# Mixture of experts on one core: tokens sorted by group on chip, and the expert weights moved past 128 sorted tokens instead of 256 tokens moved past the weights

## The reference, cut to what matters

```python
def _moe_sublayer(x, ...):                      # 256 tokens, D = 2048
    ht = _rms(x, ffn_norm_g)
    g_prob = softmax(ht @ w_router_group + b)   # 4 groups
    p_group, g_sel = top_k(g_prob, 1)           # one group for each token
    e_logit = (ht @ w_router_expert + b).reshape(T, 4, 4)[arange(T), g_sel]
    top_val, top_idx = top_k(e_logit, 2)        # two of the group's four experts
    w_top = softmax(top_val) * p_group
    ...
    for e in range(16):                         # D_EXPERT = 256
        hid = silu(ht @ w_expert_gate[e]) * (ht @ w_expert_up[e])
        y = y + combine[:, e:e + 1] * (hid @ w_expert_down[e])
    return x + y
```

## Time and profile before

| | |
|---|---|
| median of 3 runs | 3567.73 us (3565.65 to 3570.1) |
| the profiled execution: its own time | 3567.64 us |
| its span, from the first to the last instruction | 3565.8 us |
| mean granted TensorE clock | 0.988 of 2.4 GHz |
| TensorE busy | 3477.7 us, 98% of the span |
| VectorE, ScalarE busy | 1912.3 us (54%), 1482.6 us (42%) |
| HBM read | 593.76 MB, 167 GB/s over the span |

### The profile page before, as it was taken

One profiled execution on the slowest core, in us unless ns is written; L12 is line 12 of the kernel. 1 busy time (PEld: TensorE's weight loads), 2 busy tenths in 40 slices (PEclk: granted clock), 3 DMA queues, 4 the chain that ended last, 5 costly groups with the idle time before them and its releaser, 6 DMA issues.

```text
span 3565.8 us, 64376 instructions
## 1 busy us (share of the span) xinstructions
PE 3477.7 (98%) x27880; PEld 3408.4 (96%) x27880; DVE 1912.3 (54%) x1663; ACT 1482.6 (42%) x1475; POOL 184.4 (5%) x179
## 2 busy tenths in 40 slices
PE   7999989999999999999999999999999999999998
PEld 7898879999999999999999999999988999999998
DVE  6644555555555665555444444454677554545454
ACT  4334444333333467434333333443355443434342
POOL 1140001000000022010000000010000100000001
PEclk9999999899999999999999999999999999999999
DMA  6544335456555544555555555555543566656564
GB/s 187 175 142 130 119 118 165 132 186 188 186 182 186 186 136 148 171 176 179 174 174 176 177 177 175 174 171 165 176 130 111 184 189 188 185 185 186 188 188 142
DMA packets 578957, 598.24 MB, mean 168 GB/s; under 512 B 11728, under 2 KB 565968, under 8 KB 578800
## 3 DMA queue, kind: packets, MB, share of 16 engines
q1 hardware_dynamic: 574752, 588.42, 52.9%
q0 software_dynamic: 1552, 5.92, 0.6%
q10 hardware_dynamic: 2496, 1.56, 0.2%
HBM read 593.76 MB, written 2.10 MB: 167 GB/s over the span
## 4 chain that ended last, share of the span: by engine, by line
PE 87%; DVE 6%; ACT 3%; issue 2%; DMA 1%; SPq 0%; POOL 0%; ACTq 0%; DVEq 0%; POOLq 0%
PE acc L484 26%; PE acc L486 26%; PE acc L488 26%; DVE low L1442 2%; ACT high L1002 1%; PE psx L855 1%; ACT probs L1115 1%; DMA raw<-in_w_in 1%; PE psx L704 1%; PE acc L839 1%; PE psx L839 1%; PE acc L838 1%; PE psx L838 1%; PE psx L840 1%; PE acc L840 1%
## 5 line engine op out<-in xcount | busy, mean ns | idle before, releaser
L1698 DVE TENSOR_TENSOR low<-raw,high 128x2048 fp32r<-128x2048 f32 x374 | 857.1, 2292 | 573.4 <-ACT high L1181 573.1
L484 PE MATMUL acc<-gh,high 128*128 128x256 f32 (+1 forms) x5440 | 1122.0, 288 | 24.6 <-DVE low L1442 20.7
L486 PE MATMUL acc<-gl,high 128*128 128x256 f32 (+1 forms) x5440 | 1104.5, 284 | 0.0
L488 PE MATMUL acc<-gh,low 128*128 128x256 f32 (+1 forms) x5440 | 1103.4, 284 | 0.0
L1181 ACT ACTIVATE high<-raw 128x2048 fp32r<-128x2048 f32 x374 | 714.6, 1911 | 646.4 <-DMA raw<-in_mlp_w 507.8
L484 PEld LDWEIGHTS acc<-gh,high 128*128 128x128 f32 x5440 | 850.0, 190 | 35.0 <-issue 25.1
L486 PEld LDWEIGHTS acc<-gl,high 128*128 128x128 f32 x5440 | 850.1, 190 | 0.0
L488 PEld LDWEIGHTS acc<-gh,low 128*128 128x128 f32 x5440 | 845.2, 189 | 0.0
L1442 DVE TENSOR_TENSOR low<-raw,high 128x2048 fp32r<-128x2048 f32 x180 | 418.4, 2329 | 334.4 <-ACT high L1002 333.7
L1002 ACT ACTIVATE high<-raw 128x2048 fp32r<-128x2048 f32 x180 | 342.8, 1910 | 229.2 <-DMA raw<-in_w_kv 62.6
L484 PE MATMUL acc<-fh,high 128*128 128x272 f32 (+1 forms) x2048 | 414.6, 284 | 0.0
(11 more groups left out here) (339 smaller groups left out, 3052.0 us busy)
## 6 DMA issues: line engine op xcount, KB each, us to landing
raw<-in_mlp_w SPq DMA_DIRECT2D x256, 1024.0 KB, 5.5
raw<-in_w_in SPq DMA_DIRECT2D x60, 1024.0 KB, 5.2
raw<-in_a_w_in SPq DMA_DIRECT2D x40, 1024.0 KB, 5.1
raw<-in_w_expert_gate SPq DMA_DIRECT2D x32, 1024.0 KB, 5.3
raw<-in_w_expert_up SPq DMA_DIRECT2D x32, 1024.0 KB, 5.3
raw<-in_w_expert_down SPq DMA_DIRECT2D x32, 1024.0 KB, 5.4
raw<-in_w_kv SPq DMA_DIRECT2D x32, 1024.0 KB, 5.5
raw<-in_a_w_out SPq DMA_DIRECT2D x20, 1024.0 KB, 5.1
```

Source lines behind the costliest of these rows:

```text
L484: pe.matmul(o[n], hw[:, k, c[n]], h, start=first, stop=False)
L486: pe.matmul(o[n], hw[:, k, c[n]], l, start=False, stop=False)
L488: m = pe.matmul(o[n], lw[:, k, c[n]], h, start=False, stop=last)
L1698: dve.tensor_tensor(low[:, k % SLOTS, :], raw[:, k % SLOTS, :], high[:, k % SLOTS, :].bitcast(F32), ALU.subtract)\
```

## The change

- **Router earlier.** The last steps of `wout` also transpose each finished pair of tiles of `hT` (`turn_tokens`, four 128 x 128 transposes) and do the router's matmuls for it (`router(t)`). ACT takes the transposed tiles as `xth` and their squares' sums (`take_tokens`), DVE the remainders `xtl`.
- **Sort.** Before any expert: DVE picks each token's group; TensorE counts (`count`) the groups and each token's place in its own; DVE orders the groups by size, writes their numbers to `gid`, and makes a one-hot matrix from tokens to sorted places. SP reads `gid` into four registers and only then issues the first expert weights. TensorE multiplies the tokens by the one-hot matrix (`sort`, 64 matmuls of 256 columns), ACT and DVE split the result into `gsh` and `gsl`. The second largest group comes first, then the largest, which lies across the border at place 128, then the other two: so rank 0 has tokens in both halves of 128 places, and each of ranks 1, 2 and 3 in one.
- **Experts.** The 128 sorted tokens are the stationary operand and 256 columns of weights move past. A unit of rank 0 has 48 matmuls of 256 columns, a unit of ranks 1 to 3 has 24. Units come in fours, rank 0, 1, 2, 3. The hidden values come out by tokens and are transposed back (`turn_hidden`).
- **Down.** Again tokens are stationary: 24 matmuls of 512 columns for rank 0 and 12 for each other rank. The loads have rows of 4 KB instead of 1 KB. The result is taken in two halves of the columns, each put back into token order by a matmul with the transposed one-hot matrix (`unsort`, 8 calls of 8 matmuls of 256 columns) and added to `hT`.
- The first two pairs of `a_in` are worked on with their halves interleaved (`A_ORDER`), so that the second half of `hT` is needed two units later. One of the seven sums of squares (`sum_squares`, `stats`) is gone, as are `turn_weights` and `weights_out`.
- The experts and `down` are written out instead of looped.

```diff
-            with sp.Fori(0, NEXP) as i:
-                for j in range(4):
...
+            sp.wait_ge(gid_ready, 1)
+            at_rank = [sp.value_load(gid[0:1, r:r + 1], min_val=0, max_val=NGRP - 1) for r in range(4)]
+            for u in range(64):
+                k, j, q = U0["experts"] + u, u // 16, u % 16
+                sp.wait_ge(unit_done, k - SLOTS + 1)
+                sp.dma_start(raw[:, k % SLOTS, :].rearrange("p (kt n) -> p kt n", n=256),
+                             (vg if q < 8 else vu)[q // 4 % 2, :, ds(at_rank[q % 4] * EPG + j, 1), :, :]
+                             .rearrange("p e kt n -> p (e kt) n")).then_inc(raw_in[k % SLOTS], 16)
...
+        RANKS = [[(0, 0), (1, 1)], [(0, 2)], [(1, 3)], [(1, 4)]]
...
+            def count():
+                pe.wait_ge(grouped, 1)
...
+                pe.matmul(o[:, 0:4], ones[:, :], g0, start=True, stop=False)
+                pe.matmul(o[:, 0:4], ones[:, :], g1, start=False, stop=True)
+                pe.matmul(o[:, 4:8], earlier[:, :], g0, start=True, stop=True)
+                pe.matmul(o[:, 8:12], ones[:, :], g0, start=True, stop=False)
+                pe.matmul(o[:, 8:12], earlier[:, :], g1, start=False, stop=True).then_inc(count_mm, 1)
+            def sort(t):
+                for k in range(2):
+                    c = slice(P * (2 * t + k), P * (2 * t + k) + P)
+                    for n, (i, x) in enumerate(((0, xth), (1, xth), (0, xtl), (1, xtl))):
+                        m = pe.matmul(sort_bank(t)[:, S * k:S * k + S], x[:, i, c], onehot[:, i, :],
+                                      start=n == 0, stop=n == 3)
+                m.then_inc(sort_mm, 1)
...
+            def expert_unit(u):
+                k, j, q = U0["experts"] + u, u // 16, u % 16
+                part, h, r = q // 8, q // 4 % 2, q % 4
+                pe.wait_ge(lo_ready, k + 1)
...
+                for kk in range(8):
...
+                    for s, x in RANKS[r]:
+                        o = bank_of(x)[:, 256 * part:256 * part + 256]
+                        a, b = gsh[:, kt, P * s:P * s + P], gsl[:, kt, P * s:P * s + P]
+                        pe.matmul(o, a, hw[:, kk, :], start=kt == 0, stop=False)
+                        pe.matmul(o, b, hw[:, kk, :], start=False, stop=False)
+                        m = pe.matmul(o, a, lw[:, kk, :], start=False, stop=kt == KT - 1)
+                    if kk == 3:
+                        if u == 5:
+                            turn_onehot()
+                        elif u == 7:
+                            sort_values()
+                        elif q == 15:
+                            turn_hidden(5 * j), turn_hidden(5 * j + 1)
+                        elif j and q < 3:
+                            turn_hidden(5 * j - 3 + q)
+                m.then_inc(unit_done, 1)
...
+            def down_unit(u):
...
+                for f in range(2):
+                    for s, x in RANKS[r]:
+                        a, b = hidh[:, x, j, f, :], hidl[:, x, j, f, :]
...
+                        for n in range(2):
+                            pe.matmul(down_bank(c, s, n), a, hw[:, f, 512 * n:512 * n + 512], start=first, stop=False)
...
+                    elif f == 0 and 18 <= u < 22:
+                        unsort(u - 18)
...
             for u in range(40):
                 k = U0["a_in"] + u
...
+                def mid():
+                    if u == 0:
+                        for t in range(4, 8):
+                            unsort(t)
```

On DVE the start of the experts reads:

```diff
+            for t in range(4):
+                sorted_low(t)
+            lo_c(U0["experts"])
+            sorted_low(4), sorted_low(5)
+            lo_c(U0["experts"] + 1)
+            sorted_low(6), sorted_low(7)
...
+            for u in range(64):
+                j, q = u // 16, u % 16
+                lo_c(U0["experts"] + u + 2)
+                if u == 0:
+                    shares()
+                elif u == 1:
+                    slot_values()
```

More of the change, by code:

```diff
@@ L776, in router @@
[L776 to L788, removed]
-                    m = pe.transpose(psx[0:NEXP, 3, P * i:P * i + P], comb[:, i, :], ident)
-                m.then_inc(comb_t, 1)
@@ L804, in expert @@
-            def expert(i):
-                for j in range(4):
-                    k = U0["experts"] + j
-                    fresh = isinstance(i, int)
-                    unit(i * 4 + k, k % SLOTS, j % 2, 2, B0["experts"] + j // 2, lambda kt: gh2[:, kt, :],
-                         lambda kt: gl2[:, kt, :], free=i * 2 + (B0["experts"] + j // 2 - 1),
-                         need=need_g(8) if fresh and j < 2 else None, mid=turn_weights if fresh and j == 2 else None)
-                    if fresh and j == 0:
-                        router()
-                    if fresh and j >= 2:
-                        weights_out(j - 2)
@@ new lines, in router @@
+            def router(t):
+                if t == 0:
+                    pe.wait_ge(rg_ready, 1)
+                for i in range(2):
+                    for kt in (2 * t, 2 * t + 1):
+                        m = pe.matmul(psx[:, 2 + i, 0:20], hT[:, kt, META + P * i:META + P * i + P], rg[:, kt, :],
+                                      start=kt == 0, stop=kt == KT - 1)
+                if t == 7:
+                    m.then_inc(rl_mm, 1)
+            for u in range(16):
+                k, t = U0["wout"] + u, u // 2
+                def mid():
+                    if u == 0:
+                        heads_out(NKV - 1)
+                    elif u % 2 == 0:
+                        turn_tokens(t - 1), router(t - 1)
+                unit(k, k % SLOTS, u % 2, 2, B0["wout"] + t, lambda kt: yh[:, kt, :], lambda kt: yl[:, kt, :],
+                     free=B0["wout"] + t - 1, need=need_y if t == 0 else None, mid=mid)
@@ L820, in need_hid @@
+            for u in range(32):
+                down_unit(u)
             def need_hid(base):
@@ L1242, in _, with sorted_hi @@
-            expert(0)
-            with act.Fori(0, NEXP - 1) as i:
-                expert(i + 1)
-            resid_stage("down", 2, 4, 2, "g_a", gh3, ALL)
-            hi_c(U0["a_in"] + 2)
-            root(2, TB)
+            def sorted_hi(t):
+                act.wait_ge(sort_mm, t + 1)
+                for k in range(2):
+                    m = act.activation(gsh[:, 2 * t + k, :], sort_bank(t)[:, S * k:S * k + S], ACT.Copy,
+                                       scale=col("g_ffn", 2 * t + k))
+                m.then_inc(g_hi, 1)
@@ L1250, in _ @@
+            for n in range(4):
+                take_sorted(1, n)
+            hi_c(U0["a_in"] + 2)
+            for t in range(4, 8):
+                resid(t, t, t % 2, 1, 2, "g_a", gh3, ALL)
+                if t == 5:
+                    hi_c(U0["a_in"] + 3)
+            root(1, TB)
             act.wait_ge(lam_z, 1)
@@ L1822, in _ @@
+            lo_c(U0["a_in"] + 2)
+            add_back(4), add_back(5)
+            for t in range(4, 8):
+                if t < 6:
+                    add_back(t + 2)
+                g_low(t, "g_a", gh3, gl3, ALL, 16 + t + 1)
+                if t == 6:
+                    lo_c(U0["a_in"] + 3)
+            root(1, TB)
             half_log, z, s_, s2, p_ = (rc[:, k, :] for k in (0, 2, 3, 4, 5))
```

541 lines of the change are left out of this document (382 added, 159 removed).

## The result

The changed kernel takes 3429.93 us (median of 4 runs, 3429.1 to 3436.9), the kernel before took 3568.91 in runs beside it: ratio 0.9615, 95% interval 0.9601 to 0.9629. It is 139 us faster. The forecast was 3422 us, 8 us less. The profiled execution took 3430.53 us with a span of 3428.7; all that follows is read from it.

A forecast was written before the change was run, and what follows sets the result against it. TensorE, 98% busy, was taken as the bound. wout 15.0, start 52.7, other units 226.0, down 123.3 and end 5.8 make 422.8 us in place of 568.1, giving span 3420.5 and time 3422 us, range 3385 to 3480.

The forecast's parts named there:

- `wout`: `wout` stage: seven of eight tile pairs' transposes and router matmuls inside it, at 0.18 us each, add 15 us, nothing hiding them.
- start to the end of unit 4: From the last `wout` matmul through five expert units: 19.7 us of matmuls plus 33.0 bare, 52.7 us.
- the other 59 units: Gate and up after unit 4: 205.7 us of matmuls, 14.75 waits of 1.27 and 1.6 for transposes, 226.0 us.
- down: Down: eight fours of 15.24 us, each with a 1.44 us wait, plus 1.4 for `unsort` and `turn_hidden`, 123.3 us.
- end: `unsort`, recurrent block: First `a_in` units: 3.8 us for the second half of `unsort`, recurrent DVE chain about 2 us later, 5.8 us.
- The bound changes hands: Gate and up: rank 0's slot needs 9.72 us, TensorE has 8.45 of work, so it waits 1.27 us every four units.
- Rival 1: Gate, up and down: landing under 4.0 us brings slots round within 8.4, waits go, TensorE stays bound; 3392 us, chance 0.12.
- The period of four: Gate and up: four units, one of each rank, take 15.35 us including TensorE's wait for rank 0's slot.
- Bare time: Start of the experts: TensorE time not covered by the first five units' matmuls, 33 us, range 25 to 44.
- rival 2: Experts and down: the clock falls at each wait, 1.7 us in each of 24 fours; 3463 us, chance 0.15.

The follow-up runs named there:

- e8_rows: Changed kernel with gate and up loads giving each partition 8 KB of adjacent rows instead of 8 rows of 1 KB: 3415.81 us (one run).
- e6_router: Changed kernel with all 64 router matmuls behind the last matmul of `wout` instead of 8 in each pair of units: 3424.83 us (one run).
- e5_fixed: Changed kernel with expert groups in fixed order, so SyncE reads no group number into a register before the first expert load: 3431.86 us (one run).
- e1_order: Changed kernel with low passes of `a_in` units 4 and 5 ahead of root, first convolution and decay-rate chain, ScalarE's copies likewise: 3429.97 us, ratio 0.9628.
- e9_band: Changed kernel with the order of e1_order and the first group's eight band loads issued two loads later in `a_in`: 3423.94 us, ratio 0.959.
- e7_old_order: Changed kernel with the first four `a_in` units in the order of before, sum of squares after the second unit: 3429.84 us.
- e11_late: Changed kernel with each rank 0 load in gate, up and down issued one unit later, from the ninth unit on: 3536.75 us.

## Why the prediction was right, and where it was off

Span 3428.7 us against 3420.5. By the prediction's own terms:

| term | forecast, us | measured, us | difference |
|---|---|---|---|
| before `wout` | 0 | -2.6 (538.1 against 540.7) | -2.6 |
| `wout` | +15.0 | +9.0 (102.7 against 93.7) | -6.0 |
| start to the end of unit 4 | 52.7 | 47.2 | -5.5 |
| the other 59 units | 226.0 | 232.7 | +6.7 |
| down | 123.3 | 126.0 | +2.7 |
| end: `unsort`, recurrent block | +5.8 | +15.0 | +9.2 |
| after that | 0 | +3.7 | +3.7 |

- **The bound changes hands.** Right, in place, cause and size. The forecast wait was 1.27 us in every four, the mean of 13 is 1.40; the fifth slot took it away and one unit's delay lengthened it by 3.3 us where 2.8 were put in. Rival 1 needed a landing under 4.0 us; the shortest for rank 0 was 5.3 in gate and up, 5.0 in down, and 4.7 with rows of 8 KB.
- **The period of four** is 15.94 us on the mean of 13 instead of 15.35 (15.97 without the last), and most of the +6.7 is this (1.6 for transposes were counted besides). Of the 0.6 us, 0.3 are rank 0's landing, 5.56 us up to ACT's start instead of 5.25; 0.1 is SP, which issues 0.33 us after the border of the units in every other pair of fours instead of 0.19; and 0.2 are the unit of rank 0 itself, with its transposes and the one fall of the clock. The landing of 5.25 us came from the kernel before, where loads stood 5.6 us or more apart. Now three of four are issued 2.4 to 3.6 us after the one before, most of them 2.8, and with rows of 1 KB these take 5.5 to 7.8 us and rank 0's 5.3 to 5.8. e8_rows shows that the rows do it: with 8 KB rank 0's take 4.7 to 5.0. The prediction's sentence "rows of 4 KB could shorten the landing; I count nothing" was the right observation at the wrong stage: it should have been weighed for the loads that kept short rows.
- **Down.** 512 columns take 0.233 us, near the upper of the two bounds, and the wait is 0.85 to 1.33 instead of 1.44. In its second half TensorE is the bound for some 30 us, where `unsort` fills the waits; 1.6 of the 2.7 more are in that half, 1.0 in the first. This was read, not tested.
- **Wout.** Right in place, too large by 6 us: a record was priced at 0.18 us, from groups that average both clock levels. At full clock the router's matmul is 0.11 (e6_router: 6.4 us for 56). The text had named 3 us of this.
- **The start.** Unit 0 at 23.4 us (24.2 forecast), units 3 and 4 waiting behind `shares` and `slot_values` as forecast, but for 2.09 and 0.30 us where 3.1 and 2.5 were forecast. Bare time 27.5 instead of 33: 0.8 of this is unit 0, 3.2 are these two waits, and the rest is the clock, which fell once, for less than the 3 us that were added. From `gid`'s end at 651.42 to SP's first issue at 654.10 it is 2.68 us for four register loads, and hidden (e5_fixed). The Trainium skill (DMA: Bandwidth & Descriptors, Latency and other measured facts) gives a floor of about 600 ns for one; the estimate from it was 2.4 us for four, and the trace agrees.
- **The end.** Here a step of the prediction failed: "the recurrent block's DVE chain starts about 2 us later because its first pair is complete after three units". It starts 17 us later, not 2: the root's reciprocal comes 24.3 us after the first `a_in` matmul instead of 7.2. The sum of squares that it waits for was behind the first unit and is behind the third, and the first unit lasts 11.1 us instead of 6.3. And what stands behind the chain was left out: DVE has the low pass of unit 4 there, in both kernels, so TensorE waits 9.25 us where it had 0.71. Of the 15.0 us, 8.5 are this, 4.9 the longer first unit (3.8 forecast) and some 2 the clock, which falls behind the wait; a wait of 0.7 before unit 3 is gone. e1_order, e9_band and e7_old_order show that DVE's order and the band's loads hold TensorE up, one under the other.
- **After that**, 3.7 us: from 2400 to 2800 us 3080 matmuls start where 3108 did in the same stretch before, at a clock of 0.99 instead of 1.00, with the same waits. Nothing was changed there. The clock fell twice near 2600 us and did not in the trace of before, though TensorE's waits there are the same (2.01, 1.84 and 1.45 us; before 2.00, 1.94 and 1.45); 27 of the 28 matmuls are missing in these 40 us, which stand below for the changed kernel and for the one before. All 13 traces with the change have falls in this part and take 1853.7 to 1857.5 us for it; the one trace of before has none ahead of its last 12 us and takes 1852.0. Why the clock fell in the one and not in the other stays open.

```profile
2580.00:2620.00 40.00, 34.71 (x222) 31.18 (x221) 27.31 (x34) 19.66 (x31) 0.00 (x0) 0.87 0.28 87
...
2720.80:2760.80 40.00, 34.06 (x249) 30.76 (x248) 28.91 (x35) 20.37 (x32) 2.71 (x2) 1.00 0.34 106
```

- **The clock (rival 2).** It happened in one of 13 fours, 1.3 us, and in up to three of them in other traces with the same stage. That it was not more is in part luck: the mean wait of 1.40 us is clear of it, but the single waits reach 1.99, where the clock fell about every second time. e11_late shows that it falls in all at waits three times as long, and at the price that the rival had, 1.6 us a wait (1.7 forecast). The Trainium skill (TensorE: Matmul & The Clock Gate, HAM oscillation — how this bites in real kernels) tells of a kernel with M = 128 in which the clock falls at each wait for the next operand, with waits of some 3 to 5 us; the trace agrees for the 4.4 us of e11_late. The waits here are shorter than the page's, so the prediction's "by that rule the time would be 3463" took it further than it goes.

So part of the nearness of 3422 to 3430 is luck: two terms too large (11.5 us) stood against three too small (18.6).

## What to carry over

When a change takes work from the engine that is the bound, work out the round of each buffer next: release, issue, landing, conversion, use. Here it gave the new period to 4%, and one more buffer for every second of the heaviest units gave back 20 of the 25 us of waiting. A landing time read where loads stand far apart is too short for one where they follow each other, above all with short rows. And when a stage starts elsewhere than before, go through each in-order queue at its border and write down what stands ahead of the next pass that TensorE needs, and what the first of these waits for: edits there uncover one hurdle under another, so count on less than the wait that is shown.

## What the runs showed of the hardware

- Loads of 1 MB in pieces of 1 KB, three of four issued some 2.8 us apart, land after 6.3 to 6.6 us in the median, and after 5.3 where they stand 5.5 us or more apart; in pieces of 8 KB per partition, after 5.1, at a lower share of busy DMA time (0.76 instead of 0.82 over 684 to 920 us) and a higher rate (277 instead of 266 GB/s).
- Between stretches of 120 matmuls the granted clock fell to 1.2 GHz behind waits of 2.9 to 5.7 us (22 of 22), for some 15 matmuls of 256 columns; behind waits of 1.79 to 1.99 us it did in 10 of 22 cases, and behind none of 0.9 to 1.75 us.
- An fp32r matmul of 512 columns takes 0.233 us from start to start: twice that of 256 (0.117). In the changed kernel's timeline, with two records a row, the rows are 0.46 us apart:

```profile
940.31 0.63 PE L969 MATMUL acc<-low,hidh 128*128 128x512 f32 x2
940.77 0.63 PE L965 MATMUL acc<-high,hidh 128*128 128x512 f32 x2
```
